# Latent attention by pairs of heads, with the next mixer's value projection moved ahead

## The reference, cut to what matters

```python
proj = h @ w_in[l]            # c_q (384), c_kv (256), k_pe (32), sb_q, sb_k, sb_v (512 each), r_q, ...
q  = (rmsnorm(c_q, g_q) @ w_uq[l]).reshape(B, S, 8, 64 + 32)
kv = (rmsnorm(c_kv, g_kv) @ w_ukv[l]).reshape(B, S, 8, 64 + 64)
k_rot = broadcast(apply_rope(k_pe))                       # one for all 8 heads
q_a = concatenate([q[..., :64], apply_rope(q[..., 64:])])
k_a = concatenate([kv[..., :64], k_rot])
y_a = softmax(causal(q_a @ k_a.T * 96 ** -0.5)) @ kv[..., 64:]    # query blocks of 128
```

## Time and profile before

| | us |
|---|---|
| median of 3 runs | 4009.09 (4005.47 to 4017.19) |
| profiled execution | 4004.28 |
| its span | 4002.5 |
| TensorE busy | 3817.9 (95%) |
| VectorE busy | 1758.2 (44%) |
| ScalarE busy | 1494.4 (37%) |
| GpSimd busy | 252.1 (6%) |
| mean granted TensorE clock | 0.982 of full |

### The profile page before, as it was taken

The page is one execution under the profiler, slowest core; times in us unless marked ns, Lnnn a source line. Parts: engine busy times, 40 slices in busy tenths (PEclk is TensorE's granted clock), DMA queues, the critical chain, the costliest instruction groups (busy, mean ns, idle before and its releaser), DMA issues.

```text
span 4002.5 us, 45335 instructions
## 1 busy us (share of the span) xinstructions
PE 3817.9 (95%) x18892; PEld 3119.0 (78%) x18892; DVE 1758.2 (44%) x2690; ACT 1494.4 (37%) x2371; POOL 252.1 (6%) x199
## 2 busy tenths in 40 slices
PE   7998888999998999999889999999998999999998
PEld 6897777888887977788666768878876676887887
DVE  5326635544544145545454443343335444334332
ACT  4245423322323246323344533232324453323232
POOL 0000010000000000000000011120110001112011
PEclk8999999999999999999999999999999999999999
DMA  5330012333321222232211122322221112332222
GB/s 198 103 106 2 32 64 71 108 117 114 107 81 62 82 69 77 84 100 92 85 36 65 64 71 95 103 86 99 95 90 36 65 64 71 95 103 86 99 95 84
DMA packets 110430, 335.80 MB, mean 84 GB/s; under 512 B 11664, under 2 KB 28432, under 8 KB 110096
## 3 DMA queue, kind: packets, MB, share of 16 engines
q1 hardware_dynamic: 110224, 332.90, 25.0%
HBM read 329.18 MB, written 2.10 MB: 83 GB/s over the span
## 4 chain that ended last, share of the span: by engine, by line
PE 90%; DVE 5%; ACT 3%; issue 1%; DMA 1%; POOL 0%; SPq 0%; DVEq 0%; ACTq 0%
PE ps L579 66%; PE ps L615 6%; PE ps L598 2%; PE ps L663 2%; PE ps L1098 1%; PE ps L1134 1%; PE ps L624 1%; PE ps L807 1%; PE ps L1021 1%; PE ps L1009 1%; PE ps L1000 1%; PE ps L972 1%; PE ps L834 1%; PE ps L1052 1%; DMA raw<-weights_d 1%
## 5 line engine op out<-in xcount | busy, mean ns | idle before, releaser
L2031 DVE TENSOR_TENSOR wlo<-raw,whi 128x1024 fp32r<-128x1024 f32 (+3 forms) x655 | 746.7, 1144 | 1026.6 <-ACT whi L1297 1025.7
L1297 ACT ACTIVATE whi<-raw 128x1024 fp32r<-128x1024 f32 (+3 forms) x655 | 628.0, 969 | 811.6 <-PE ps L579 636.1
L579 PE MATMUL ps<-bh,whi 128*128 128x512 f32 x1248 | 493.5, 395 | 0.1
L579 PE MATMUL ps<-bh,wlo 128*128 128x512 f32 x1248 | 486.2, 390 | 0.8 <-DVE wlo L2031 0.8
L579 PE MATMUL ps<-bl,whi 128*128 128x512 f32 x1248 | 486.0, 389 | 0.0
L579 PE MATMUL ps<-ah,whi 128*128 128x512 f32 (+2 forms) x1424 | 420.6, 354 | 13.8 <-ACT whi L1297 13.8
L579 PE MATMUL ps<-ah,wlo 128*128 128x512 f32 (+2 forms) x1424 | 418.2, 353 | 0.9 <-DVE wlo L2031 0.8
L579 PE MATMUL ps<-al,whi 128*128 128x512 f32 (+2 forms) x1424 | 416.0, 351 | 0.0
L579 PEld LDWEIGHTS ps<-ah,whi 128*128 128x128 f32 x1424 | 245.7, 189 | 51.8 <-ACT whi L1297 15.9
L579 PEld LDWEIGHTS ps<-bh,whi 128*128 128x128 f32 x1248 | 234.3, 188 | 57.9 <-issue 7.1
L579 PEld LDWEIGHTS ps<-bh,wlo 128*128 128x128 f32 x1248 | 234.3, 188 | 51.0 <-DVE wlo L2031 1.7
(11 more groups left out here) (343 smaller groups left out, 6313.3 us busy)
## 6 DMA issues: line engine op xcount, KB each, us to landing
raw<-weights_d SPq DMA_DIRECT2D x543, 512.0 KB, 3.3
raw<-weights_d SPq DMA_DIRECT2D x48, 256.0 KB, 2.6
raw<-weights_d SPq DMA_DIRECT2D x48, 192.0 KB, 2.4
x<-nab_d SPq DMA_DIRECT2D x24, 256.0 KB, 2.8
x<-x_t_d SPq DMA_DIRECT2D x4, 1024.0 KB, 6.1
dt<-rtab_d SPq DMA_DIRECT2D x16, 256.0 KB, 2.8
raw<-weights_d SPq DMA_DIRECT2D x16, 128.0 KB, 2.0
out_d<-x SPq DMA_DIRECT2D x4, 512.0 KB, 2.9
```

The costliest lines, as they stand in the source:

```text
L579: m = e.matmul(p[:, 0:n], tiles(w, i)[:, k, :], xs[:, x0 + k, c0:c0 + n], start=pi == 0 and k == 0 and ti == 0, stop=i == job and k == kt ...
L1297: e.activation(flat(WHI, j), raw(j), ACT.Copy).then_inc(q.did("hi", j))
L2031: e.tensor_tensor(flat(WLO, j), raw(j), flat(WHI, j).bitcast(F32), ALU.subtract).then_inc(q.did("lo", j))
```

## The change

- Heads go in pairs. One tile holds the 64 unrotated query columns of two heads (`QN`), one their key columns (`KN`). The rotated query parts are projected for four heads at once (`QR`, two groups), 32 rows for each, and rotated in one go; the key part `KR` holds the same 32 rows four times. Eight uq and eight ukv chunks become four and four, and two uq chunks for the rotated parts.
- An item is a pair and a query block: 16 items. Its scores are four matmuls: 64 rows for each head into two banks, then 32 rows for each on top. VectorE copies the scores to SBUF with the mask added and the maximum taken, in one instruction per head. Transposes come two items later, values of both heads, in turn, three items later.
- The value projection of the stick-breaking attention comes before the key rotation, right behind the latents' projections, and its result goes into a part of `X` that is free by then. Its first query and key projections come between the last items.
- GpSimd builds a mask of 512 columns per layer.

The diff, cut to its core:

```diff
@@ weight_plan
-        S("w_in_2", (l,), 0, 8, [("z", 0, 64), ("c", 640, 32), ("z", 0, 32)], next(turn))
+        S("w_in_2", (l,), 0, 8, [("c", 640, 32)] * 4, next(turn))
+        moving("w_in_2", (l,), D, IN_OFF[5], 512, (0, 1, 2, 3))
+
+        def rope_queries(g):
+            S("mla_w_uq_2", (l,), 0, 3, [("c", 96 * h + 64, 32) for h in range(4 * g, 4 * g + 4)], (7,))
+
+        def pair(j):
+            S("mla_w_uq_2", (l,), 0, 3, [("c", 96 * h, 64) for h in (2 * j, 2 * j + 1)], (7,))
+            S("mla_w_ukv_2", (l,), 0, 2, [("c", 128 * h, 64) for h in (2 * j, 2 * j + 1)], (7 if j else 5,))
+
+        rope_queries(0)
         S("mla_w_ukv_2", (l,), 0, 2, [("c", 128 * h + 64, 64) for h in range(8)], (0, 1, 2, 3))
-        for h in range(8):
-            S("mla_w_uq_2", (l,), 0, 3, [("c", 96 * h, 96), ("z", 0, 32)], (6,))
-            S("mla_w_ukv_2", (l,), 0, 2, [("c", 128 * h, 64), ("z", 0, 64)], (7,))
-        moving("w_in_2", (l,), D, IN_OFF[5], 512, (0, 1, 2, 3))
+        for j in range(4):
+            pair(j)
+            if j == 1:
+                rope_queries(1)
...
@@ TensorE
             q.note(f"end_latent{l}", "pe")
+            lin_tok("w_in_2", B, br, 4, TOK4)
             rotate(6, ("kr", l), PM, KR, ("cq", l, 5))
...
+            def m_scores(n):
+                j, i = MLA_ITEMS[n]
+                own, w = slice(128 * i, 128 * i + 128), 128 * (i + 1)
+                ps = [bank(2 * (n % 2) + b, ("am", l, n, b)) for b in range(2)]
+                q.wait_ge(("mqn", l, j), ("mkn", l, j), ("mq", l, j // 2), ("kr", l))
+                for b in range(2):
+                    r = slice(64 * b, 64 * b + 64)
+                    e.matmul(ps[b][:, 0:w], QN[j % 2][r, own], KN[j % 2][r, 0:w], start=True, stop=False, skip_group_check=True)
+                for b in range(2):
+                    r = slice(64 * (j % 2) + 32 * b, 64 * (j % 2) + 32 * b + 32)
+                    m = e.matmul(ps[b][:, 0:w], QR[j // 2][r, own], KR[r, 0:w], start=False, stop=True, skip_group_check=True)
+                m.then_inc(q.did("as", l, n))
...
+            rope = m_rope(0)
+            next(rope)
+            lin_tok("mla_w_ukv_2", C, cr, 1, TOK4, 3)
+            next(rope, None)
+            m_queries()
+            m_keys()
+            for n in range(16 + 3):
+                if n < 16:
+                    m_scores(n)
+                if 0 <= n - 2 < 16:
+                    m_turn(n - 2)
+                if n in (16, 17):
+                    lin("w_in_2", B, br, ONE)
+                if n >= 3:
+                    m_values(n - 3)
+                j, i = divmod(n, 4)
+                if j < 3 and i == 0:
+                    m_queries()
+                if j < 3 and i == 1:
+                    m_keys()
+                if j == 0 and i == 2:
+                    rope = m_rope(1)
+                    next(rope)
+                if j == 0 and i == 3:
+                    next(rope, None)
 
             q.note(f"end_mla{l}", "pe")
-            lin_tok("w_in_2", B, br, 4, TOK4)
...
-            for _ in range(2):
-                lin("w_in_2", B, br, ONE)
             for j in range(4):
                 sb_scores(j)
...
@@ ScalarE
+            for g in range(4):
+                i = chunk("w_in_2")
+            for ti, b in enumerate(plan[i][6]):
+                q.wait_ge(("mm", i), *f)
+                e.activation(sv(ti), PS[b].rearrange("p (a k) -> p a k", a=2), ACT.Copy).then_inc(q.did("ev", i, ti))
...
+            for n in range(16 + 4):
+                if n >= 4:
+                    m_values(n - 4)
+                if n < 16:
+                    m_weights(n)
+                if 0 <= n - 2 < 16:
+                    m_turn(n - 2)
+                if n == 16:
+                    sb_queries(0)
+                if n == 17:
+                    sb_keys(0)
...
@@ VectorE
+            for _ in range(4):
+                chunk("w_in_2")
             rotate(6, ("kr", l), KR, COSM, SINM, TMP[1], *f2)
...
+            def m_keys(j):
                 i = chunk("mla_w_ukv_2")
+                q.wait_ge(("mm", i), *(f2 if j < 2 else [("as", l, 4 * j - 5)]))
+                e.tensor_copy(KN[j % 2], PS[plan[i][6][0]]).then_inc(q.did("ev", i, 0))
...
+            def m_scores(n):
+                w = 128 * (MLA_ITEMS[n][1] + 1)
+                for b in range(2):
+                    q.wait_ge(("as", l, n), ("mmask", l), *([("at", l, n - 3, b)] if n >= 3 else f2))
+                    e.tensor_tensor_reduce(m_tile(MP, n, b)[:, 0:w], PS[2 * (n % 2) + b][:, 0:w], MMASK[:, TL - w:], -1.0, 3.0e38,
+                                           ALU.add, ALU.min, NSTAT[n % 8][:, b:b + 1]).then_inc(q.did("am", l, n, b))
...
+            for n in range(16 + 4):
+                if n < 16:
+                    m_scores(n)
+                if n >= 4:
+                    m_values(n - 4)
+                if 0 <= n - 1 < 16:
+                    m_weights(n - 1)
...
@@ GpSimd
+            e.memset(MMASK[:, 0:384], 0.0).then_inc(q.did("mmask0", l))
+            e.tensor_copy(MMASK[:, 384:512], CAUSAL).then_inc(q.did("mmask", l))
             rotate(("kr", l), KR, COSM)
-            for h in range(8):
-                rotate(("mq", l, h), RAWQ[h % 2], COSM)
+            for g in range(2):
+                rotate(("mq", l, g), QR[g], COSM)
```

More of the change, by code:

```diff
@@ L263, in shape_constants @@
     pm = np.zeros((128, 128), f)
-    for d in range(64, 96):
-        if d < 80:
+    for d in range(128):
+        if d % 32 < 16:
             pm[d + 16, d] = -1
@@ L524, in build @@
     KIND = (0, 1, 1, 2)
[L525 to L526 removed]
+    MLA_ITEMS = [(j, i) for j in range(4) for i in range(4)]
     def sb_sp(h):
@@ L945, in pe_program @@
         conv_ffn(0, SEGS, iter(()), ada_beside(FILL_FFN))
[L949 to L976, removed]
         q.note("end_ffn0", "pe")
@@ L1078, in mla_head, with m_queries, m_keys @@
+            def m_queries():
+                lin("mla_w_uq_2", C, cr, ONE, ((3, 0),))
+            def m_keys():
                 lin("mla_w_ukv_2", C, cr, ONE, ((2, 3),))
[L1079 to L1092, removed]
@@ L1817, in m_beside @@
[L1817 to L1825 removed]
+            m_queries(0)
+            chunk("mla_w_ukv_2")
+            for n in range(16 + 4):
[9 more added lines that the diff above has]
+                    sb_keys(0)
+                j, i = divmod(n, 4)
+                if j < 3 and i == 0:
+                    m_queries(j + 1)
+                if j < 3 and i == 1:
+                    chunk("mla_w_ukv_2")
+                if j == 0 and i == 2:
+                    m_rope(1)
@@ new lines, in dve_program @@
+            rope = m_rope(0)
+            next(rope)
+            chunk("mla_w_ukv_2")
+            next(rope, None)
+            chunk("mla_w_uq_2")
+            m_keys(0)
+            for n in range(16 + 4):
[5 more added lines that the diff above has]
+                    m_weights(n - 1)
+                if n in (16, 17):
+                    chunk("w_in_2")
+                j, i = divmod(n, 4)
+                if j < 3 and i == 0:
+                    chunk("mla_w_uq_2")
+                if j < 3 and i == 1:
+                    m_keys(j + 1)
+                if j == 0 and i == 2:
+                    rope = m_rope(1)
+                    next(rope)
+                if j == 0 and i == 3:
+                    next(rope, None)
@@ L2576, in dve_program @@
             q.note(f"end_mla{l}", "dve")
             f = fence(f"end_mla{l}")
-            for _ in range(4):
-                chunk("w_in_2")
             def sb_scores(h):
```

224 lines of the change are left out of this document (94 added, 130 removed).

## The result

The changed kernel takes 3951.45 us (median of 4 runs, 3947.81 to 3952.44), the kernel before 4008.76 us beside it: a ratio of 0.9852, 95% interval 0.9835 to 0.9869. It is 57.3 us faster; 84.6 us were forecast, and the time lies 7 us above the range.

What follows compares the result with a forecast made beforehand. TensorE was taken as the bound (95% busy). Layer 0 gains 38.2 + 2.4 + 0.1 = 40.7 us, layer 1 39.8 + 4.0 + 0.1 = 43.9, together 84.6: forecast 3924 us, range 3912 to 3944.

Steps and rivals of the forecast that it cites:

- Does the loop keep its pace?: Head loop: about 4.1 us of cover against 3.4 us to the second scaled tile, so waits cost nothing.
- the sign of being wrong: Prediction wrong if ScalarE or VectorE ends most of TensorE's waits in the loop, or time is gained elsewhere.
- The clock: Latent-attention loop: the old dips to 1.2 GHz go, counted within gains of 38.2 and 39.8 us; no dip inside.
- Rival (d): Loop at 1.2 GHz because half-array matmuls with switches count as little work: slower, 4063 us; chance 0.02.
- rival (b): Exponential and scaling chain sets the loop's pace in places, about 1 us for each of eight items: 3932 to 3936 us; chance 0.09.
- Before the loop: Square sum to first scores: moving the 21.9 us value projection into the 3.43 us hole gains 2.4 and 4.0 us.
- Values of two heads for one: Loop: two heads on two array halves cost one, 1.02 us for four key chunks; half the values saved, 8.5 us.
- Rival (a): Loop scores: 32-row parts of two heads don't overlap, 8.5 us more per layer: 3941 us; chance 0.12.
- Six rotations and 42 projections: Loop: 42 of the layer's 120 uq/ukv matmuls (9.6 us) and six of eight rotations (5.1 us) are taken away.
- The change from 64 to 32 rows: Scores of each loop item: switch costs 0.10 us, with ends at 0 and 0.30 us.
- A projection inside the loop: Three further pairs of 9 + 6 matmuls in the loop: 45 x 0.228 + 0.6 = 10.9 us.
- Behind the loop: Stick-breaking projections between last turns and values gain 0.7 us; the exponential chain starts some 0.6 us later: net 0.1 per layer.

Runs made afterwards that it cites:

- experiment 1: The changed kernel with VectorE taking the low part of the pair's output ahead of the next item's scores; 3936.6 us.
- experiment 2: The changed kernel with two useless fp32 matmuls of 384 columns on TensorE at each wait for the output bank; 3935.3 us.
- experiment 5: Experiment 1's kernel with ScalarE's copies of turned tiles put ahead of the next item's exponentials; 3928.0 us.
- experiment 8: Experiment 5's kernel without the 32-row matmuls of the rotated parts, so scores are incomplete; 3916.9 us.
- e1_order: The same run as experiment 1: the changed kernel with VectorE's low part of the output ahead of the next item's scores; 3936.6 us.
- e7_both_orders: The same run as experiment 5: experiment 1's kernel with ScalarE's turned-tile copies ahead of the next exponentials; 3928.0 us.
- e12_weights_first: Experiment 5's kernel with last square sum inside the values, rotated parts on 64 rows, and VectorE scaling the last weights before the next masked copies; 3925.8 us.

## Why the prediction was wrong, by its own steps

**The failed step** is "Does the loop keep its pace?", and in it the sentence that costs the waits at nothing. It followed one chain, from scores to scaled tile, and found 4.1 us of cover for 3.4 us. That chain never ended a wait in the changed kernel: VectorE's low part of the output ended all six, which is the sign of being wrong that the prediction named. What it left out are the waits on banks: the values of a new pair on the one output bank, emptied by VectorE behind two copies (1.43 us, three times a layer), and, hidden behind that wait and seen in experiment 1, the transposes on bank 4, emptied by ScalarE behind two exponentials (0.82 to 1.67 us). The change has an added wait there: `bank(6, ("aol", ...))` was a wait on banks 4 and 5 in turn. The prediction did not name it, and took the pace from a stage that has two output banks. Cost: 8.6 us.

**The clock** was counted as a gain: the old dips would go, and none come. Rival (d) named the lower clock, but put it down to the shapes. The dips follow TensorE's standing still: 34.1 us at half clock in the two loops, gone in experiment 2 where only the idle time was filled, and with them 15.0 us of loop. The prediction's sentence that waits cost "about 1 us for each" in rival (b), 3932 to 3936 us, had no price for the clock behind them; that is the largest mis-sized term, more than half of the gap.

**The gap in sum.** In the two stretches of the table, 85.8 us were forecast (84.6 and the 0.6 us a layer that were to be lost behind them), and 57.7 us came: 28.1 us too few. The waits make 8.6 us of it, the clock 15.0 by experiment 2, and the loop's own work 4.2: in experiment 5, with no dip and its waits taken out, it is 71.6 us and not 69.5, in each layer. That leaves 0.3 us.

**What held.** Before the loop: 37.0 us against 37.1; 0.88 us for the key tile against 1.0, and 1.60 us ahead of the squares against 1.6. Values of two heads for one: four chunks in 1.03 us. Rival (a): the groups of 32 rows overlap in full, 1.06 us for c = 4 of both heads (2105.01 to 2106.07 above), where one after the other would be 1.7. Six rotations and 42 projections went. The chain that the prediction watched does lie close below TensorE: experiment 8 brings it up, with 3.7 us of waits for scaled tiles.

**Smaller terms.** The change from 64 to 32 rows costs 0.20 us, not 0.10: 3.2 us in both layers. The prediction's own rows pointed there: in the earlier trace rows the steps of 1.06, 1.03 and 1.02 us for four chunks leave 0.17 to 0.21 us for each change. (Those three shapes are that stage's; the latent attention before had two per item, 128 rows and then 64 columns.) A projection inside the loop costs 0.23 us above its columns (nine matmuls 2.28, six 1.59), not 0.10: about 1 us a layer. Together that is about 2.6 us a layer, somewhat more than the 2.1 us by which the loop without waits exceeds the forecast. Behind the loop, the hole of the stick-breaking chain did not grow by 0.6 us (1.21 us before, 1.24 after): ScalarE's copy of the last output fits into the 2.4 us of scores.

**Elsewhere.** The profiled executions differ by 53.2 us in span, not 57.7: the changed kernel's is 2.3 us later already at the latents for reasons ahead of the change, and loses 2.2 us more in the parts behind the two loops. The two programs are the same there; where the dips fall is not. Outside the two stretches the changed kernel's trace has 131.2 us at half clock, the one before 121.0.

## What to carry to other kernels

When two stages are compared because they have the same form, compare their PSUM banks too: for each bank, who empties it, and what is queued ahead of the emptying on that engine. Put the step that frees a shared bank ahead of steps that have slack, on every engine in the chain; two exchanged pairs of calls were worth 23.5 us here (3951.5 to 3928.0; 21.0 us in the loops), beside the 57.3 us of the whole rewrite. And price a wait of TensorE twice: by its own length, and by what the clock does behind it.

## What the runs showed of the hardware that was not expected

- Waits of 1.43 us, three in 40 us, were followed by up to 10.2 us at 1.2 GHz of full work. The six cost 8.6 us of waiting and 15.0 us of clock. Filling them with matmuls that nobody uses made the kernel 16.2 us faster. Not each wait does it: those of 0.82 to 1.67 us in e1_order were followed by two dips in layer 0 and none in layer 1, 1.08 us in e7_both_orders by none, and 1.45 us in e12_weights_first by none. What decides it is not shown.
- A change from 64-row to 32-row tiles costs 0.20 us even though the same two PSUM banks go on being summed up; two groups of 64 rows in a row cost nothing at their border (0.74 + 0.75 us; 6 chunks are 1.28 us, which leaves 0.21 for one switch).
- Tiles of 32 rows (at rows 0 and 32, for odd pairs at 64 and 96) overlap as fully as two halves do: 1.06 us for c = 4 of either kind.
